# MLP up units in pairs of seven half-token products, with the down halves between them

## The chip, the cores and the metric

The kernel runs on one core of one Trainium2 chip. The time is device microseconds of one execution. The profiled execution is a run of its own, recorded by the hardware profiler.

## The reference

Two transformer blocks of different kinds on 512 tokens of width 1024, in float32. The first block (two layers: four-branch mixing and a gated FFN) is not touched. The second has a recurrent layer, a layer of banded attention, and behind each an MLP of this form, with 1024 inputs and 4096 hidden outputs:

```python
def rmsnorm_2(x, g):
    xf = x.astype(jnp.float32)
    y = xf * lax.rsqrt(jnp.mean(xf * xf, axis=-1, keepdims=True) + EPS)
    return (y * g.astype(jnp.float32)).astype(x.dtype)

def sqrelu_mlp(x, w_up, w_down):
    return jnp.square(jax.nn.relu(x @ w_up)) @ w_down

h = h + sqrelu_mlp(rmsnorm_2(h, mlp_norm[l]), w_up[l], w_down[l])     # l = 0, 1
```

## The kernel before

All weights lie in memory as 476 units of 128 x 1024 floats (512 KB): for most units eight 128 x 128 blocks, the weights of 128 outputs against 1024 inputs. Everything is transposed: a tile has 128 features on the partitions and 512 tokens in the columns. `X` holds the eight tiles of the residual. Float32 accuracy is made of three float32r products: `three` computes high x high, high weight x low value, low weight x high value, so a unit is 8 x 3 = 24 matmuls of 512 columns into one PSUM bank of `ps`.

A unit passes these stations, each engine in program order:
- SyncE loads it into one of four slots of `w_raw` when the unit four before has been used (`w_used`).
- ScalarE rounds it to `w_hi` (`split_weights`, L433; `tick(u)` does unit u + 2).
- GpSimd makes `w_lo` = raw - high in two halves of 512 (`low`, L368 and L370), in place of the raw weights.
- TensorE multiplies (`unit`, with `three` at L902 to L904), by `H_hi`, `H_lo` (the normed input) or `Y_hi`, `Y_lo` (the hidden tiles).
- ScalarE or DVE takes the bank away (`unit_out`).

An MLP (`mlp(n, U0)` on each engine) is four quarters of 8 up units and 8 down units. For an up unit ScalarE does the relu from PSUM to `fa` (L819), DVE multiplies by the row of inverse roots `RS` (L1980), squares it into `XS` (L1981), ScalarE rounds that to `Y_hi` (L821), DVE makes `Y_lo` (L1984). For a down unit DVE adds the bank to `X` (L1992). The gain is in `H`; the norm's root comes late, so RS is applied behind the up product: the norm is a matmul after unit 0 (L1026), a root on ScalarE (L477) and a reciprocal on DVE (L1484). Ahead of an MLP the eight output units of the layer are added to `X` (L1964 in the first), DVE sums the squares (L1476) and ScalarE and DVE make `H_hi` and `H_lo` (L455, L1489). The first block's scores (L1170) and the norm's sums per token (L1042) are plain float32 matmuls.

The middle quarters of an MLP run in a hardware loop on every engine, with the waits computed from the loop's counter. All order is written by hand.

Of the kernel before, what the change touches and what calls it, by code (L numbers as in the profile page):

```python
# [20 lines left out]
UNIT = 8 * P  # L21
WSLOTS = 4
# [16 lines left out]
QUARTERS = 4  # L39
U_AIN, U_AGATE, U_AOUT = 16, 2, DT  # L40
# [44 lines left out]
def build(nc, xT, w_all, vecs, cossin, win_fix, pool_w, sgu_wT, sgu_b, sgu_g, bias2, outT):  # L85
# [67 lines left out]

    o_rs2 = room(2 * KB)
# [26 lines left out]
    with ctx:  # L181
# [39 lines left out]
        stored = sem("stored")  # L221

# [96 lines left out]

        block = ctx.enter_context(nc.Block())  # L320
# [24 lines left out]
        def _(eng):  # L345
# [37 lines left out]
            def pooled(name):  # L383
# [12 lines left out]
                eng.sem_inc(sq_pooled, 1)  # L396
            at = 0
# [4 lines left out]
            lows(at, UO)  # L402
# [24 lines left out]
        def _(act):  # L427
# [374 lines left out]
            for k in range(3, DT):  # L802
                lru_hi(k)
            for k in range(1, DT):
                tick(UAO + k)
                x_tile("mlp0", "a_out")(k - 1)

            def mlp(n, U0):
# [4 lines left out]
                def quarter(i, first, last):  # L813
                    for j in range(8):
                        u = i * 16 + (U0 + j)
                        if j or not first:
                            tick(u, U0 + j)
                        act.wait_ge(w_used, u + 1)
                        nc.scalar.activation(fa[:, j % 2, :], ps[:, (U0 + j) % 4, :], ACT.Relu).then_inc(f_act, 1)  # L819
                        act.wait_ge(src_ready, i * 8 + (SRC[f"mlp{n}"] + j + 1))  # L820
                        nc.scalar.activation(Y_hi[:, j, :], XS[:, j % 2, :], ACT.Copy).then_inc(hi_ready, 1)  # L821
                    if last and n == 0:
                        tick_and_split(i * 16 + (U0 + 8), x_tile("kv_norm", "mlp0"))
                        return
# [73 lines left out]
        def _(pe):  # L898
            MM = nc.tensor.matmul

            def three(out, wh, wl, xh, xl, start, stop):
                MM(out, wh, xh, start=start, stop=False)  # L902
                MM(out, wh, xl, start=False, stop=False)  # L903
                return MM(out, wl, xh, start=False, stop=stop)  # L904
# [432 lines left out]

            def mlp(n, U0):
                def quarter(i, first):
                    for j in range(8):  # L1340
                        unit(i * 16 + (U0 + j), U0 + j, ps[:, (U0 + j) % 4, :], Hh, Hl, 8, i * 16 + (U0 + j - 3),
                             SPLIT[f"mlp_in{n}"] if first and j == 0 else None)
                        if first and j == 0:
                            norm(f"mlp{n}")
                    for m in range(8):
                        c = U0 + 8 + m
                        unit(i * 16 + c, c, ps[:, c % 4, :], Yh, Yl, 8, i * 16 + (c - 3), None if m else i * 8 + SPLIT[f"mlp{n}"])
                quarter(0, True)
                with pe.Fori(1, QUARTERS) as i:
                    quarter(i, False)  # L1350
# [880 lines left out]
```

## Time and profile before

| | us |
|---|---|
| median of three runs | 2755.32 (2753.72 to 2759.18) |
| profiled execution | 2752.11 |
| its span | 2750.4 |
| TensorE busy | 2708.3, 12398 matmuls |
| DVE, ScalarE, GpSimd busy | 1215.4, 1061.8, 1323.3 |

Granted TensorE clock over the span: 0.998. The kernel moves 259 MB at a mean of 94 GB/s. The first MLP runs from 1767 to about 2120 us, the second from about 2397 to the end. The records of TensorE are pipelined: a matmul of 512 columns is recorded with 0.39 us, so the distance of two starts is its cost, not its duration.

### The profile page before, as it was taken

The numbers are of one execution on the slowest core, as the hardware profiler recorded it, in microseconds if no ns is written. First come the engines' busy times: TensorE is split into PE (matmuls) and PEld (weight loads), VectorE is DVE, ScalarE is ACT, GpSimd is POOL, SyncE is SP. The second block draws the span as 40 slices with busy tenths as digits, with TensorE's granted clock in tenths as the row PEclk, the third lists the DMA queues.
The fourth block names the chain that finished last, engine by engine and source line by source line (L and its number), as shares of the span: only waits on it lengthen the run. The fifth ranks groups of instructions, "written<-read, shape, count | busy, mean of one in ns | idle before, by whom it ended". The sixth has DMA issues, their size and how long they took to land.

```text
span 2750.4 us, 34272 instructions
## 1 busy us (share of the span) xinstructions
PE 2708.3 (98%) x12398; PEld 2203.9 (80%) x12398; DVE 1215.4 (44%) x1603; ACT 1061.8 (39%) x1566; POOL 1323.3 (48%) x1028
## 2 busy tenths in 40 slices
PE   9999999999999999999999999999999998999999
PEld 7777787888877788787888877788888876788887
DVE  6755555222258645555121268633324237343222
ACT  4444434222343444434222348423324338433222
POOL 5455445544465545455444465454444432354443
PEclk9999999999999999999999999999999999999999
DMA  4233322233233333322323322223223220223233
GB/s 144 93 102 97 99 92 85 95 97 100 93 100 100 98 95 99 100 92 85 100 93 99 100 92 92 92 92 100 92 98 122 85 77 16 69 92 100 93 98 99
DMA packets 72699, 259.16 MB, mean 94 GB/s; under 512 B 8192, under 2 KB 9088, under 8 KB 72448
## 3 DMA queue, kind: packets, MB, share of 16 engines
q1 hardware_dynamic: 71280, 254.17, 29.0%
q10 hardware_dynamic: 1296, 3.28, 0.3%
q8 instruction: 87, 1.43, 0.2%
q14 instruction: 36, 0.29, 0.0%
HBM read 255.31 MB, written 2.10 MB: 94 GB/s over the span
## 4 chain that ended last, share of the span: by engine, by line
PE 67%; issue 13%; POOL 10%; DVE 5%; ACT 2%; DMA 1%; POOLq 0%; DVEq 0%; SPq 0%
PE ps L902 20%; PE ps L904 20%; PE ps L903 20%; POOL w_lo L370 6%; POOL w_lo L368 5%; PE ps L1170 1%; DVE XS L1981 1%; ACT w_hi L433 1%; DMA w_raw<-w_all 1%; DVE fb L1980 1%; PE ps L1065 1%; DVE st L1545 1%; PE ps L936 1%; PE ps L930 1%; PE ps L931 1%
## 5 line engine op out<-in xcount | busy, mean ns | idle before, releaser
L368 POOL TENSOR_TENSOR w_lo<-w_raw,w_hi 128x512 fp32r<-128x512 f32 x476 | 634.4, 1333 | 1327.1 <-ACT w_hi L433 1326.3
L902 PE MATMUL ps<-H_hi,w_hi 128*128 128x512 f32 x2160 | 858.4, 397 | 9.9 <-POOL w_lo L370 5.7
L904 PE MATMUL ps<-H_hi,w_lo 128*128 128x512 f32 x2160 | 841.4, 390 | 0.0
L903 PE MATMUL ps<-H_lo,w_hi 128*128 128x512 f32 x2160 | 841.0, 389 | 0.0
L433 ACT ACTIVATE w_hi<-w_raw 128x1024 fp32r<-128x1024 f32 x476 | 499.6, 1055 | 552.1 <-DMA w_raw<-w_all 551.8
L370 POOL TENSOR_TENSOR w_lo<-w_raw,w_hi 128x512 fp32r<-128x512 f32 x476 | 654.6, 1375 | 0.0
L902 PEld LDWEIGHTS ps<-H_hi,w_hi 128*128 128x128 f32 x2160 | 405.5, 188 | 109.8 <-issue 14.4
L903 PEld LDWEIGHTS ps<-H_lo,w_hi 128*128 128x128 f32 x2160 | 405.6, 188 | 89.2 <-issue 7.4
L904 PEld LDWEIGHTS ps<-H_hi,w_lo 128*128 128x128 f32 x2160 | 405.4, 188 | 85.3
L902 PE MATMUL ps<-Y_hi,w_hi 128*128 128x512 f32 x1168 | 457.8, 392 | 7.4 <-DVE Y_lo L1693 2.8
L904 PE MATMUL ps<-Y_hi,w_lo 128*128 128x512 f32 x1168 | 455.2, 390 | 0.0
L903 PE MATMUL ps<-Y_lo,w_hi 128*128 128x512 f32 x1168 | 454.9, 389 | 0.0
L902 PEld LDWEIGHTS ps<-Y_hi,w_hi 128*128 128x128 f32 x1168 | 219.6, 188 | 55.4 <-DVE Y_lo L1693 3.2
L904 PEld LDWEIGHTS ps<-Y_hi,w_lo 128*128 128x128 f32 x1168 | 219.5, 188 | 46.2
L903 PEld LDWEIGHTS ps<-Y_lo,w_hi 128*128 128x128 f32 x1168 | 219.7, 188 | 44.9
L1980 DVE TENSOR_TENSOR fb<-fa,RS 128x512 f32<-128x512 f32 x64 | 63.3, 989 | 147.0 <-ACT fa L819 113.3
L1992 DVE TENSOR_TENSOR X<-X,ps 128x512 f32<-128x512 f32 x48 | 33.0, 688 | 207.5 <-PE ps L904 207.5
L1813 DVE TENSOR_TENSOR XS<-fb,ps 128x512 f32<-128x512 f32 x44 | 30.3, 688 | 188.2 <-PE ps L904 177.8
L682 ACT ACTIVATE Y_hi<-XS 128x512 fp32r<-128x512 f32 x44 | 27.8, 632 | 218.3 <-DVE XS L1815 218.3
L1619 DVE TENSOR_TENSOR G<-ps,RS 128x512 f32<-128x512 f32 x64 | 44.3, 691 | 134.7 <-PE ps L904 132.8
L538 ACT ACTIVATE G<-G 128x512 f32<-128x512 f32 x64 | 40.3, 631 | 160.5 <-DVE G L1619 160.3
L821 ACT ACTIVATE Y_hi<-XS 128x512 fp32r<-128x512 f32 x64 | 40.5, 632 | 141.1 <-DVE XS L1981 141.1
(284 smaller groups left out, 2589.9 us busy)
## 6 DMA issues: line engine op xcount, KB each, us to landing
w_raw<-w_all SPq DMA_DIRECT2D x476, 512.0 KB, 3.5
X<-xT SPq DMA_DIRECT2D x8, 256.0 KB, 5.5
rel_bias<-bias ACTq DMA_DIRECT2D x1, 2048.0 KB, 8.9
outT<-X SPq DMA_DIRECT2D x8, 256.0 KB, 3.0
sguw<-sgu_wT ACTq DMA_DIRECT2D x2, 256.0 KB, 3.2
CS<-cossin SPq DMA_DIRECT2D x1, 256.0 KB, 7.7
sgub<-sgu_b ACTq DMA_DIRECT2D x2, 128.0 KB, 3.1
sgug<-sgu_g ACTq DMA_DIRECT2D x2, 128.0 KB, 3.2
```

The lines of the kernel that those rows point to most:

```text
L368: nc.gpsimd.tensor_tensor(w_lo[:, s, 0:UNIT // 2], w_raw[:, s, 0:UNIT // 2], f(w_hi[:, s, 0:UNIT // 2]), ALU.subtract).then_inc(w_lo_half, 1)
L370: nc.gpsimd.tensor_tensor(w_lo[:, s, UNIT // 2:UNIT], w_raw[:, s, UNIT // 2:UNIT], f(w_hi[:, s, UNIT // 2:UNIT]), ALU.subtract).then_inc(w ...
L433: nc.scalar.activation(w_hi[:, c % WSLOTS, :], w_raw[:, c % WSLOTS, :], ACT.Copy).then_inc(w_hi_ready, 1)
L538: nc.scalar.activation(dst, dst, ACT.Sigmoid).then_inc(sig_done, 1)
L821: nc.scalar.activation(Y_hi[:, j, :], XS[:, j % 2, :], ACT.Copy).then_inc(hi_ready, 1)
L902: MM(out, wh, xh, start=start, stop=False)
L903: MM(out, wh, xl, start=False, stop=False)
L904: return MM(out, wl, xh, start=False, stop=stop)
L1619: VE.tensor_tensor(dst, ps[:, bank(o), :], RS[:], ALU.mult).then_inc(g_lin, 1)
L1813: lk(VE.tensor_tensor(XS[:, j % 2, :], fb[:, j % 2, :], ps[:, (u0 + 2 * j + 1) % 4, :], ALU.mult))
L1980: lk(VE.tensor_tensor(fb[:, 0, :], fa[:, j % 2, :], RS[:], ALU.mult))
L1992: VE.tensor_tensor(X[:, m, :], X[:, m, :], ps[:, c % 4, :], ALU.add).then_inc(unit_out, 1)
```

## The change

In each MLP the first four up units stay as they are. The other 28 are taken in 14 pairs. Two units of 128 outputs, each with two halves of 512 inputs, against the two halves of 256 tokens, are a 2 x 2 block product: eight half products, made here of seven (Winograd's form of Strassen's scheme). For that,
- DVE makes four sums of weight halves a pair (S1 to S4, `weight_sum`), ScalarE their high parts (`hi_sum`), GpSimd their low parts, in `E_raw`, `E_hi`, `E_lo`;
- once for an MLP DVE makes four sums of token halves (`token_sums`, T0 to T3), the first two tiles of them between the additions of the layer before; their high parts are ScalarE's, their low parts DVE's (T3, T0) and GpSimd's (T1 ahead of the first pair, T2 behind it);
- partial results are copied from PSUM to `cp` by ScalarE and added by DVE (`c11`, `c12`, `c2`), then one DVE step does relu and RS, and ScalarE squares twice, into `XS` and `Y_hi`.

Down units hold two outputs against 4 input tiles each, and are computed as four half downs a window, two of them between the half products. A window is one pair of up units and two down units. At the end the down units of outputs 0 to 5 come as pairs of halves, 6 and 7 as whole units. The order of w_all follows. The rest of the kernel stays. The core of the diff, TensorE first:

```diff
+            def half_product(bank, wh, wl, xh, xl, fresh=True):
+                for k in range(4):
+                    c = slice(k * P, (k + 1) * P)
+                    m = three(ps[:, bank, 0:HS], wh[:, c], wl[:, c], xh(k), xl(k), fresh and k == 0, k == 3, not fresh)
+                return m
             def mlp(n, U0):
-                def quarter(i, first):
-                    for j in range(8):
-                        unit(i * 16 + (U0 + j), U0 + j, ps[:, (U0 + j) % 4, :], Hh, Hl, 8, i * 16 + (U0 + j - 3),
...
+                def window(i, w, first=False, last=False):
...
+                    half_product(BANK_Q, *slot_part(c + 1, 1), *half_of_h(4, 0))
...
+                    half_product(BANK_G, *slot_part(c, 1), *tokens(3)).then_inc(w_used, 1)
...
+                    half_product(BANK_R, *slot_part(c + 1, 0), *half_of_h(0, 0)).then_inc(w_used, 1)
...
+                    half_product(BANK_V, *sum_part(w, S1_), *tokens(0)).then_inc(st_mm, 1)
+                    if not (first or last):
+                        half_down(0)
+                    pe.wait_ge(st_lo, q * 3 + 1)
+                    pe.wait_ge(st_copy, q * 4 + 2)
...
+                    half_product(BANK_R, *sum_part(w, S2_), *tokens(1), fresh=False).then_inc(st_mm, 1)
+                    pe.wait_ge(st_lo, q * 3 + 2)
+                    pe.wait_ge(st_copy, q * 4 + 3)
+                    half_product(BANK_V, *sum_part(w, S4_), *half_of_h(4, 1), fresh=False).then_inc(st_mm, 1)
+                    if not (first or last):
+                        half_down(1)
+                    pe.wait_ge(st_lo, q * 3 + 3)
+                    pe.wait_ge(st_copy, q * 4 + 4)
...
+                    half_product(BANK_R, *sum_part(w, S3_), *tokens(2), fresh=False).then_inc(st_mm, 1)
+                    if not last:
+                        for d in range(0 if first else 2, 4):
+                            half_down(d)
```

ScalarE, one window and the start of an MLP:

```diff
+                def window(i, w, last=False):
+                    hi_unit(i, w, 3)
+                    copied(i, w, COPY_G)
+                    copied(i, w, COPY_R1)
+                    copied(i, w, COPY_V)
+                    if last:
+                        hi_unit(i, w, 4)
+                        hi_unit(i, w, 5)
+                    else:
+                        hi_second(i, w + 1)
+                        hi_unit(i, w, 5)
+                        hi_sum(i, w + 1, S1_)
+                        hi_sum(i, w + 1, S2_)
+                    copied(i, w, COPY_R2)
+                    if not last:
+                        hi_sum(i, w + 1, S4_, 2)
+                    squared(i, w, 0)
+                    if not last:
+                        hi_unit(i, w, 6)
+                    squared(i, w, 1)
...
+                relu(0)
+                tick(U0 + 1)
+                hi_tokens(3, 0)
+                relu(1)
+                up_hi(0)
+                hi_second(0, 0)
+                hi_unit(0, 0, 1)
+                hi_sum(0, 0, S1_)
+                hi_sum(0, 0, S2_)
+                hi_tokens(1)
+                hi_sum(0, 0, S4_, 2)
+                up_hi(1)
+                relu(2)
+                hi_unit(0, 0, 2)
+                up_hi(2)
+                hi_tokens(2)
+                relu(3)
+                up_hi(3)
+                for w in range(4):
+                    window(0, w)
```

DVE, one window and the start; GpSimd, the low parts of a pair:

```diff
+                def window(i, w, first=False, last=False):
+                    c11(i, w)
+                    if not last:
+                        weight_sum(i, w + 1, S1_)
+                        weight_sum(i, w + 1, S2_)
+                        if not first:
+                            down(i, w, 0)
+                        weight_sum(i, w + 1, S4_)
+                        weight_sum(i, w + 1, S3_)
+                    c12(i, w)
+                    linear(i, w, 0)
+                    if not (first or last):
+                        down(i, w, 1)
+                    low(i, w, 0)
+                    c2(i, w)
+                    linear(i, w, 1, 0 if first or last else 1)
...
+                token_sums(n, 2)
+                token_sums(n, 3)
                 link(root(f"mlp{n}", RS[:]))
...
+                up(0)
+                for o in (S1_, S2_):
+                    weight_sum(0, 0, o)
+                low_tokens(3, 1)
+                for o in (S4_, S3_):
+                    weight_sum(0, 0, o)
+                low_tokens(0, 2)
+                up(1)
+                up(2)
+                up(3)
```

```diff
+            def low_pair(n, U0, i, w):
...
+                eng.wait_ge(st_sum, q * 4 + 3)
+                nc.gpsimd.tensor_tensor(w_lo[:, s1, S:UNIT], w_raw[:, s1, S:UNIT], f(w_hi[:, s1, S:UNIT]), ALU.subtract).then_inc(w_lo_half, 1)
+                eng.wait_ge(st_sum, q * 4 + 4)
+                nc.gpsimd.tensor_tensor(w_lo[:, s2, S:UNIT], w_raw[:, s2, S:UNIT], f(w_hi[:, s2, S:UNIT]), ALU.subtract).then_inc(w_lo_half, 1)
+                nc.gpsimd.tensor_tensor(w_lo[:, s1, 0:S], w_raw[:, s1, 0:S], f(w_hi[:, s1, 0:S]), ALU.subtract).then_inc(w_lo_ready, 1)
+                for m, o in enumerate((S1_, S2_, S4_, S3_)):
```

## Rows read from the trace of the kernel before

**Rows 1.** The page: TensorE's busy time, and the chain that ended last, by engine.

```profile
PE 2708.3 (98%) x12398; PEld 2203.9 (80%) x12398; DVE 1215.4 (44%) x1603; ACT 1061.8 (39%) x1566; POOL 1323.3 (48%) x1028
...
PE 67%; issue 13%; POOL 10%; DVE 5%; ACT 2%; DMA 1%; POOLq 0%; DVEq 0%; SPq 0%
```

**Rows 2.** Windows view inside the first MLP: length, busy time and records of each engine.

```profile
core 0: us, PE busy (x) PEld busy (x) DVE busy (x) ACT busy (x) POOL busy (x), PEclk, DMA share, GB/s
...
1800.00:2100.00 300.00, 298.94 (x1319) 247.23 (x1318) 95.06 (x119) 94.91 (x120) 143.54 (x112) 1.00 0.30 96
```

**Rows 3.** TensorE's waits from 1700 us on: us in total, times, longest.

```profile
PE ps L902 <- DVE Y_lo L1984: 2.1, 2, 1.1
```

**Rows 4.** Timeline: start us, duration us; additions to X, then matmuls and loads.

```profile
1851.20 0.69 DVE L1992 TENSOR_TENSOR X<-X,ps 128x512 f32<-128x512 f32 x1 [4.75 <-PE ps L904]
1856.64 0.69 DVE L1992 TENSOR_TENSOR X<-X,ps 128x512 f32<-128x512 f32 x1 [4.75 <-PE ps L904]
...
1499.87 0.39 PE L902 MATMUL ps<-Y_hi,w_hi 128*128 128x512 f32 x1
1500.10 0.39 PE L903 MATMUL ps<-Y_lo,w_hi 128*128 128x512 f32 x1
...
1499.87 0.19 PEld L903 LDWEIGHTS ps<-Y_lo,w_hi 128*128 128x128 f32 x1
```

**Rows 5.** Timeline of the first block's float32 scores, by windows cut between the records.

```profile
112.23 0.38 PE L1170 MATMUL ps<-Kh,Qh 128*128 128x128 f32 x2
...
112.45 0.92 PE L1170 MATMUL ps<-Kh,Qh 128*128 128x256 f32 x3
...
112.67 0.70 PE L1170 MATMUL ps<-Kh,Qh 128*128 128x256 f32 x2
...
112.89 0.81 PE L1170 MATMUL ps<-Kh,Qh 128*128 128x384 f32 x2
```

**Rows 6.** Timeline of one-column float32 matmuls with a full weight load each.

```profile
435.97 0.47 PE L1042 MATMUL ps<-ones,SQ 128*128 128x1 f32 x3
...
436.42 0.36 PE L1042 MATMUL ps<-ones,SQ 128*128 128x1 f32 x2
```

**Rows 7.** Timeline of DVE and GpSimd in the first MLP's first quarter.

```profile
1781.76 1.28 DVE L1980 TENSOR_TENSOR fb<-fa,RS 128x512 f32<-128x512 f32 x1 [0.86 <-ACT fa L819]
1783.08 1.67 DVE L1981 TENSOR_TENSOR XS<-fb 128x512 f32<-128x512 f32 x1
...
1781.20 1.29 POOL L368 TENSOR_TENSOR w_lo<-w_raw,w_hi 128x512 fp32r<-128x512 f32 x1 [8.30 <-ACT w_hi L433]
1782.45 1.74 POOL L370 TENSOR_TENSOR w_lo<-w_raw,w_hi 128x512 fp32r<-128x512 f32 x1
```

**Rows 8.** Groups by line, 1800 to 2100 us, and the DMA issue to landing.

```profile
L370 POOL TENSOR_TENSOR w_lo<-w_raw,w_hi 128x512 fp32r<-128x512 f32 x56 | 73.8, 1319 | 0.0
...
L433 ACT ACTIVATE w_hi<-w_raw 128x1024 fp32r<-128x1024 f32 x57 | 59.6, 1052 | 96.7 <-DMA w_raw<-w_all 96.7
...
L1984 DVE TENSOR_TENSOR Y_lo<-XS,Y_hi 128x512 fp32r<-128x512 f32 x28 | 19.4, 693 | 20.2 <-ACT Y_hi L821 20.2
L821 ACT ACTIVATE Y_hi<-XS 128x512 fp32r<-128x512 f32 x28 | 17.7, 632 | 56.3 <-DVE XS L1981 56.3
...
w_raw<-w_all SPq DMA_DIRECT2D x55, 512.0 KB, 3.5
```

**Rows 9.** Timeline and chain where the first MLP begins.

```profile
1767.37 0.69 DVE L1964 TENSOR_TENSOR X<-X,ps 128x512 f32<-128x512 f32 x1 [2.39 <-PE ps L904]
...
1769.49 0.75 DVE L1489 SCALAR_TENSOR_TENSOR H_lo<-X,V,H_hi 128x512 fp32r<-128x512 f32 x1
1774.40 3.35 DVE L1484 RECIPROCAL RS<-SQ 128x512 f32<-128x512 f32 x1 [4.16 <-ACT SQ L477]
...
1772.71 0.88 PE ps L1026 x2
```

**Rows 10.** Groups by form, whole span: half-width operations on DVE and ScalarE.

```profile
L1755 DVE SCALAR_TENSOR_TENSOR vnT<-ps,st,sgug 128x256 f32<-128x256 f32 x8 | 3.9, 484 | 0.3
...
L619 ACT ACTIVATE SQ<-ps 128x256 f32<-128x256 f32 x8 | 3.1, 386 | 14.5 <-PE ps L1241 14.3
```

More of the change, by code:

```diff
@@ L21 @@
 UNIT = 8 * P
+HS = S // 2
+S1_, S2_, S4_, S3_ = range(4)
+COPY_G, COPY_R1, COPY_V, COPY_R2 = range(4)
+BANK_Q, BANK_G, BANK_V, BANK_R = 4, 5, 6, 7
 WSLOTS = 4
@@ L420, in _ @@
                     low(UO + 2 + (h > 4), 2 + (h > 4))
-            with eng.Fori(UO // WSLOTS + 1, NU // WSLOTS) as i:
-                for s in range(WSLOTS):
-                    low(i * WSLOTS + s, s)
+            lows(UO + 4, UM1 + 4)
+            low_mlp(1, UM1)
         @block.scalar
@@ new lines, in mlp @@
+                hi_tokens(1)
[7 more added lines that the diff above has]
+                up_hi(3)
+                for w in range(4):
+                    window(0, w)
+                with act.Fori(1, QUARTERS - 1) as i:
+                    for w in range(4):
+                        window(i, w)
+                window(QUARTERS - 1, 0)
@@ L833, in _ @@
+                window(QUARTERS - 1, 1, True)
+                split_weights(U0 + 62, U0 + 62)
+                for k in range(7):
+                    if n == 0:
+                        x_tile("kv_norm", "mlp0")(k)
+                    if k in (1, 3, 5):
+                        split_weights(U0 + 63 + k // 2, U0 + 63 + k // 2)
             mlp(0, UM0)
@@ new lines, in c11, with c12 @@
+                def c11(i, w):
+                    dve.wait_ge(st_copy, pair_at(n, i, w) * 4 + 2)
+                    VE.tensor_tensor(fa[:, 0, 0:HS], ps[:, BANK_Q, 0:HS], cp[:, COPY_R1, :], ALU.add).then_inc(st_c, 1)
+                def c12(i, w):
+                    q = pair_at(n, i, w)
+                    dve.wait_ge(st_copy, q * 4 + 4)
+                    dve.wait_ge(st_mm, q * 4 + 3)
+                    VE.tensor_tensor(fa[:, 0, HS:S], ps[:, BANK_V, 0:HS], cp[:, COPY_R2, :], ALU.add).then_inc(st_c, 1)
@@ new lines, in mlp @@
+                token_sums(n, 2)
+                token_sums(n, 3)
+                link(root(f"mlp{n}", RS[:]))
+                up(0)
[8 more added lines that the diff above has]
+                up(3)
+                for w in range(4):
+                    window(0, w, first=w == 0)
@@ new lines, in mlp @@
+                with dve.Fori(1, QUARTERS - 1) as i:
+                    for w in range(4):
+                        window(i, w)
+                window(QUARTERS - 1, 0)
+                window(QUARTERS - 1, 1, last=True)
+                for m, b in enumerate((2, 3, BANK_Q, BANK_G, 0, 1, 2, 3)):
+                    if m < 6 and m % 2 == 0:
+                        dve.wait_ge(d_mm, down_half(n, QUARTERS - 1, 1, 0) + m // 2)
+                    else:
+                        dve.wait_ge(w_used, U0 + (60 + m // 2 if m < 6 else 57 + m))
+                    VE.tensor_tensor(X[:, m, :], X[:, m, :], ps[:, b, :], ALU.add).then_inc(x_done, 1)
+                    dve.wait_ge(x_done, XDONE[f"mlp{n}"] + m + 1)
+                    if m not in (2, 4):
+                        dve.sem_inc(unit_out, 1)
```

339 lines of the change are left out of this document (271 added, 68 removed).

## Prediction

> **What bounds the kernel now.** I read the page's busy shares and chain first, then TensorE's windows inside the first MLP, then its waits, then the single starts. TensorE is busy 2708.3 of 2750.4 us, and two thirds of the chain that ends last is its matmuls [rows 1]. In the 300 us window inside the first MLP it is busy 298.94 us at granted clock 1.00, which is the 2.4 GHz level [rows 2]. All that the MLPs lose to a named wait is 2.1 us, one wait of about 1.1 us in each, where the first down unit needs the last part of `Y_lo` [rows 3]. So inside the MLPs the time is the number of matmuls times their spacing, and the change can gain only there.
>
> The spacing: two additions of down results to `X` start 5.44 us apart, one unit of 24 matmuls of 512 columns, 0.2267 us each. The records start 0.23 apart, and the load for the next matmul starts with the one before it and is hidden [rows 4]. 512 columns at 2.4 GHz are 0.2133, so each matmul carries 13 ns beyond its columns. A unit costs 5.44, a pair of up units 10.88 us.
>
> **What the change removes and adds on TensorE.** Per MLP four up units stay whole and 14 pairs are rewritten (28 pairs in all). A pair was 48 matmuls of 512 columns. It becomes seven half-token products of 4 contraction tiles x 3 parts = 84 matmuls of 256 columns. Down work is the same number of matmuls, regrouped. The price of one 256-column float32r matmul, c, decides: break-even is 10.88/84 = 129.5 ns. No such matmul is in the trace. Bounds:
> - From below: the scores of the first block are plain float32 and take two records a matmul, two clocks a column. Their 128-column records have the same time on the moving side (256 clocks, 107 ns) and a full 128x128 load each. Two of them take 112.23 to 112.45, 0.11 each; the 256-column ones next take 0.22 [rows 5]. One-column matmuls with a full load start 0.45/4 = 0.1125 apart [rows 6]: load and issue alone allow no less than 0.11.
> - Float32r's 13 ns: if it goes with the columns, c = 0.2267/2 = 0.1135. If it is a fixed price of each matmul, c = 0.1067 + 0.0133 = 0.120.
> - From above: if load and moving reads share something, so that time goes with 128 loaded + N moving elements, 640 elements now take 226.7 and 384 would take 136 ns.
>
> I take 0.120: the plain float32 records of three widths exceed their columns by about 3 ns whatever the width [rows 5], so a fixed price is the form that this trace shows. A pair is then 84 x 0.120 = 10.08, 0.80 saved; 28 pairs save 22.4 us. With 0.1135 it is 9.53, 37.8 saved; with 0.136 it is 11.42, 15 us lost.
>
> The records show loads hidden and short ones at 0.11 [rows 5, 6]. The Trainium skill ("TensorE: Matmul & The Clock Gate", Back-to-back issue gap) says that the single-matmul gap under-counts at small N in a stream of load and matmul pairs, 81 ns measured against 56 at N = 128. Were the same 25 ns added to its 262 cycles at N = 256, an estimate from that page, c would be 134 ns and the change would lose; no 256-column float32r stream is here to settle it.
>
> **The steady pair window, other engines.** A window of TensorE is 7 x 1.44 + 4 half downs x 2.72 = 20.96 us (two up units and two down units cost 21.76 before). GpSimd now makes 11 low parts of 512 a window (three halves of raw weights, four sums, four down halves), 8 before. DVE gets four weight sums, two linear steps, two `Y_lo`, four additions to `X` and four half-width additions; ScalarE about 10.3 us of work at 1.05 a unit and 0.63 a tile [rows 8]. DVE work with two SBUF inputs and GpSimd exclude each other: at the start of the MLP the square XS takes 1.67 instead of 0.69, exactly the rest of GpSimd's operation plus 0.56, and GpSimd's next takes 1.74 instead of 1.29 [rows 7]. GpSimd's two parts of a unit start 1.25 apart. The shared time is 11 x 1.25 + 8 x 0.5 = 17.8 us of 20.96, so it fits. The Trainium skill ("SBUF — State Buffer", on the shared port pair) calls it an exclusive lock for a whole instruction, for DVE operations with two SBUF inputs; the rows agree.
>
> I walked one window. Slots 0 and 1 come free at 2.9 and 4.3 us and land 3.5 later [rows 8]; ScalarE's high parts end at 8.9; the sums on DVE at 10.7; GpSimd makes the next window's seven low parts by 21.2 and the two parts for slot 2 by 24.2, 3.2 us into the next window, where its first half down starts at 5.8. The copies of banks G, R and V are done by 6.3, before 8.5. The chain of the second unit (sum, linear, square, low) ends 0.7 into the next window, used at 5.8. So no wait of TensorE in a steady window. That cover holds while 17.8 stays below 21; if GpSimd were the bound, each us of excess costs 28.
>
> **Where an MLP begins.** Here the new work meets on DVE and GpSimd. In trace time: unit 0 ends at 1772.7, the norm matmul takes 0.88 [rows 9], and three units of 5.44 end at 1789.9. DVE is done with the last `H_lo` at 1770.2 [rows 9]. Now come eight token sums of 256 columns at 0.48 [rows 10], two held up by GpSimd operations at 1770.4 to 1772.9: until 1776. The reciprocal of 3.35 [rows 9], which stood right behind the root, ends at 1779.5 (1777.8 before). up(0) 2.8, S1, S2, the low part of T3 (1024 wide, about 1.2) and S4: about 1786. From here GpSimd has the low part of T1 (2.5), seven parts of the first pair and T2 (2.5) ready without a gap; DVE has S3, T0 and eight steps up to the square of up(3), all with two SBUF inputs. By their order and [rows 7] they alternate at 1.25 + 0.5 = 1.75 a pair, so up(3)'s square ends near 1805.8. ScalarE is in order: only behind `up_hi(3)` (0.6) and `hi_unit` (1.05) come COPY_G and COPY_R1 (0.4 each by the 256-column row [rows 10]), done near 1808.3. TensorE waits for COPY_R1 ahead of the S2 product. It gets there near 1798 (1.4 late for the first low half, 1.0 for the next ones) and stands for 10.3 us. The S3 product waits for COPY_R2, which is queued behind the next pair's splits: 2.2 more. Sum 15 us, against 1.1 of before, in each MLP. If GpSimd held nothing up, the same chain would end at about 1798 and the sum would be 5 to 6.
>
> **Where an MLP ends.** The last window has no half downs between its products, and COPY_R2 stands behind two unit splits: ScalarE has them at 8.9 and the copy at 9.3, TensorE wants it at 8.4: 0.9 us. The last pair's Y chain (2 half additions, linear, two squares, low: about 4 us) lies beside one down unit of 5.44. Outputs 0 to 5 come 2.72 apart instead of 5.44, while DVE needs 2.9 each with the norm's steps, 1767.37 to 1770.24 [rows 9]; two full units at the end take the backlog up. Nothing for the reordering itself; the last two outputs come as before. The token sums inside the a_out and b_out units lie in DVE's idle time (over 2 us a unit [rows 9]).
>
> **Sum.** -22.4 + 2 x (15 - 1.1) + 2 x 0.9 = +7.2 us. The profiled execution took 2752.1 us (1.7 more than its span), 3.2 under the median of 2755.3; from the middle of both, 2753.7, I forecast 2761.
>
> **The rivals.**
> 1. The 13 ns goes with the columns, c = 0.1135: -37.8 + 29.6 = -8 us, faster, 2746. For it: the row's overhead is float32r's alone, and that type reads twice the elements in the same time. Against: the fixed 3 ns.
> 2. The start costs less: DVE or GpSimd do not alternate strictly, or the sums come earlier. 6.5 instead of 15: with c = 0.120 it is -22.4 + 10.8 + 1.8 = -10 us, 2744. For it: 10 of the 15 us hang on one in-order ScalarE queue. Against: [rows 7].
> 3. The narrow matmul costs over 0.125 (load and moving side in each other's way). Break-even with the start's loss is c = 0.117 ((10.88 - 29.6/28)/84); from there each ns costs 2.35 us. At 0.130 it is +30, 2784; at 0.136 +45. For it: nobody here runs a full load with 107 ns of float32r. Against: [rows 5, 6].
> 4. That the change does not do what it says (pairs that wait on each other): counted within 3.
>
> **How the numbers follow.** Forecast 0.38, rival 1 0.33, rival 2 0.13, rival 3 0.16. A measurement tells 0.2%, 5.5 us, from none. The forecast (+7, give or take 5) is faster 0.02, same 0.10, slower 0.26 of it; rival 1 (-8, give or take 5) 0.24, 0.08, 0.01; rival 2 0.09, 0.04, 0; rival 3 slower 0.16. Sums: 0.35, 0.22, 0.43. The likeliest's own range is 2753 to 2770. The range for 8 in 10 goes from rivals 1 and 2 together in part (-17) to a c of 0.129 (+28): 2737 to 2782.
>
> **What would show it.** The start distance of the new 256-column matmuls (0.120 against 0.1135 and 0.13); window length 21.0 us; TensorE's waits on ScalarE's `cp` near the start of each MLP, 10 us in one piece; DVE `XS` and sums at 1.2 to 1.7 there; no waits on `w_lo` or `E_lo` later. Wrong would be c off by more than 3 ns, a start that costs under 8, or waits in every window.

## The result, and the profile after

| | before | after |
|---|---|---|
| median, us | 2754.99 (2751.26 to 2759.18, 9 runs) | 2762.89 (2761.62 to 2766.03, 9 runs) |
| profiled execution, span | 2752.11, 2750.4 | 2763.11, 2761.4 |
| granted TensorE clock | 0.998 | 0.991 |

The ratio is 1.0031, 95% interval 1.0021 to 1.0042: slower, by 7.9 us. The page of the changed kernel:

```profile
PE 2702.9 (98%) x13406; PEld 2246.8 (81%) x13406; DVE 1403.9 (51%) x1863; ACT 1155.3 (42%) x1778; POOL 1501.3 (54%) x1116
...
PE 66%; issue 14%; POOL 11%; DVE 5%; ACT 2%; DMA 1%; POOLq 0%; SPq 0%; DVEq 0%; ACTq 0%
```

TensorE is busy 5.4 us less than in [rows 1], for 1008 more matmuls, but the span is 11 us longer. Of these, 0.8 us lie ahead of everything that was changed: the first matmul of the first MLP starts at 1767.90, against 1767.10 before. Its records where one window ends and where the next one ends (start us, duration us):

```profile
1890.29 0.39 PE L1085 MATMUL ps<-Y_hi,w_lo 128*128 128x512 f32 x1
1890.51 0.28 PE L1083 MATMUL ps<-H_hi,w_hi 128*128 128x256 f32 x1
1890.62 0.28 PE L1084 MATMUL ps<-H_lo,w_hi 128*128 128x256 f32 x1
1890.74 0.28 PE L1085 MATMUL ps<-H_hi,w_lo 128*128 128x256 f32 x1
...
1911.53 0.28 PE L1083 MATMUL ps<-H_hi,w_hi 128*128 128x256 f32 x1
```

The 256-column matmuls start 0.12 us apart, and a whole window takes 1911.53 - 1890.51 = 21.02 us. The same four units cost 4 x 5.44 = 21.76 before [rows 4]. So the steady part gains 28 x 0.74 = 20.7 us. TensorE's waits from 1700 us on (us in total, times, longest) show what is given back; [rows 3] had 2.1 us here:

```profile
PE ps L1083 <- issue: 16.1, 2, 8.9
...
PE ps L1083 <- POOL w_lo L456: 4.8, 2, 4.1
PE ps L1083 <- ACT cp L938: 3.2, 2, 1.9
```

All of this lies where the MLPs begin (4.1 and 7.3 us in the first, 0.8 and 8.9 in the second) and end (1.4 and 1.9). The windows view of the first MLP's start, with the columns of [rows 2]; the granted clock is the third number from the end:

```profile
1785.00:1790.00 5.00, 5.00 (x24) 4.14 (x23) 4.09 (x7) 4.32 (x6) 0.12 (x1) 1.00 0.31 105
1790.00:1795.00 5.00, 0.92 (x5) 0.42 (x3) 5.00 (x3) 1.06 (x1) 5.00 (x3) 0.86 0.35 107
1795.00:1800.00 5.00, 5.00 (x23) 5.00 (x24) 4.02 (x4) 2.06 (x3) 5.00 (x4) 0.50 0.00 0
1800.00:1805.00 5.00, 3.38 (x27) 3.18 (x25) 3.67 (x4) 2.06 (x3) 5.00 (x4) 0.96 0.54 165
1805.00:1810.00 5.00, 0.00 (x0) 0.00 (x0) 4.20 (x3) 1.58 (x3) 5.00 (x4) 0.73 0.11 45
1810.00:1815.00 5.00, 4.36 (x24) 4.39 (x25) 4.28 (x5) 3.70 (x8) 4.58 (x3) 0.59 0.01 2
```

TensorE stands idle for 4.1 us, and then five microseconds run at clock 0.50, the 1.2 GHz level: 23 matmuls instead of the 42 that 0.12 would allow. It stands for 7.3 us, and the clock is at 0.59 again. The start distances there are 0.21 to 0.22. Counted from the distances of all starts from 1780 to 1835 and 2410 to 2465, 75 matmuls are slowed, by 7.7 us in all.

The balance: -20.7 (windows) + 19.0 (21.1 of waits at the starts, less the 2.1 of before) + 3.3 (ends) + 7.7 (clock) = +9.3 us. Measured between the medians: +7.9; between the two profiled executions +11.0, of which 10.2 lie behind the start of the first MLP.

What TensorE waited for is seen on VectorE and GpSimd. First the timelines of both at the first MLP's start, then ScalarE's and one record of TensorE:

```profile
1756.95 1.40 DVE L2236 SCALAR_TENSOR_TENSOR T_raw<-X,V,T_raw 128x256 f32<-128x256 f32 x1
1758.27 1.51 DVE L2237 SCALAR_TENSOR_TENSOR T_raw<-X,V,T_raw 128x256 f32<-128x256 f32 x1
...
1771.93 0.75 DVE L1752 SCALAR_TENSOR_TENSOR H_lo<-X,V,H_hi 128x512 fp32r<-128x512 f32 x1
1772.71 0.48 DVE L2235 SCALAR_TENSOR_TENSOR T_raw<-X,V,T_raw 128x256 f32<-128x256 f32 x1
1773.23 1.38 DVE L2236 SCALAR_TENSOR_TENSOR T_raw<-X,V,T_raw 128x256 f32<-128x256 f32 x1
...
1780.27 3.34 DVE L1747 RECIPROCAL RS<-SQ 128x512 f32<-128x512 f32 x1
...
1790.45 3.38 DVE L2251 TENSOR_TENSOR T_lo<-T_raw,T_hi 128x1024 fp32r<-128x1024 f32 x1
...
1805.68 2.71 DVE L2258 TENSOR_TENSOR XS<-fb 128x512 f32<-128x512 f32 x1
...
1789.88 2.86 POOL L470 TENSOR_TENSOR T_lo<-T_raw,T_hi 128x1024 fp32r<-128x1024 f32 x1 [10.33 <-ACT T_hi L978]
1792.70 2.25 POOL L456 TENSOR_TENSOR w_lo<-w_raw,w_hi 128x512 fp32r<-128x512 f32 x1
...
1798.29 6.81 POOL L463 TENSOR_TENSOR E_lo<-E_raw,E_hi 128x512 fp32r<-128x512 f32 x4
...
1808.42 0.63 ACT L952 ACTIVATE Y_hi<-XS 128x512 fp32r<-128x512 f32 x1 [4.06 <-DVE XS L2258]
1808.96 1.04 ACT L525 ACTIVATE w_hi<-w_raw 128x1024 fp32r<-128x1024 f32 x1
1809.90 0.91 ACT L938 ACTIVATE cp<-ps 128x256 f32<-128x256 f32 x3
...
1810.64 0.55 PE L1083 MATMUL ps<-T_hi,E_hi 128*128 128x256 f32 x1 [7.26 <-issue]
```

From 1790 to 1808 VectorE and GpSimd mostly work by turns. The copies stand on ScalarE behind the rounding of up(3)'s square and the weight split (L525) after it. TensorE is free for its S2 product at 1803.4 and starts it at 1810.64. The profile names no releaser there ("issue"); that it is the copy, the second of three from 1809.90, is read from the times, and experiment 1 tests it.

### The profile page after: what moved, and what is told of

Its sections match the earlier page's. It is cut to its first block, busy times and chain, and to the rows that moved or that the text cites. A ratio compares the mean times of both kernels' runs of the same rounds, so it can differ in the third digit from the quotient of the medians.

```text
span 2761.4 us, 36893 instructions
## 1 busy us (share of the span) xinstructions
PE 2702.9 (98%) x13406; PEld 2246.8 (81%) x13406; DVE 1403.9 (51%) x1863; ACT 1155.3 (42%) x1778; POOL 1501.3 (54%) x1116
## 4 chain that ended last, share of the span: by engine, by line
PE 66%; issue 14%; POOL 11%; DVE 5%; ACT 2%; DMA 1%; POOLq 0%; SPq 0%; DVEq 0%; ACTq 0%
PE ps L1083 20%; PE ps L1084 19%; PE ps L1085 19%; POOL w_lo L423 5%; POOL w_lo L421 4%; DMA w_raw<-w_all 1%; PE ps L1351 1%; PE ps L1246 1%; DVE st L1808 1%; PE ps L1117 1%; PE ps L1111 1%; DVE ACC L1739 1%; PE ps L1112 1%; PE ps L1237 1%; DVE H_lo L1752 1%
## 5 line engine op out<-in xcount | busy, mean ns | idle before, releaser
L421 POOL TENSOR_TENSOR w_lo<-w_raw,w_hi 128x512 fp32r<-128x512 f32 x420 | 564.6, 1344 | 1048.0 <-ACT w_hi L525 1047.6
L1083 PE MATMUL ps<-H_hi,w_hi 128*128 128x512 f32 (+1 forms) x1936 | 748.2, 386 | 14.0 <-POOL w_lo L423 5.6
L1085 PE MATMUL ps<-H_hi,w_lo 128*128 128x512 f32 (+1 forms) x1936 | 731.0, 378 | 0.0
L1084 PE MATMUL ps<-H_lo,w_hi 128*128 128x512 f32 (+1 forms) x1936 | 730.7, 377 | 0.0
L525 ACT ACTIVATE w_hi<-w_raw 128x1024 fp32r<-128x1024 f32 x448 | 471.7, 1058 | 598.2 <-DMA w_raw<-w_all 597.7
L423 POOL TENSOR_TENSOR w_lo<-w_raw,w_hi 128x512 fp32r<-128x512 f32 x420 | 581.7, 1385 | 0.0
L1083 PEld LDWEIGHTS ps<-H_hi,w_hi 128*128 128x128 f32 x1936 | 365.0, 189 | 98.4 <-issue 13.9
L1084 PEld LDWEIGHTS ps<-H_lo,w_hi 128*128 128x128 f32 x1936 | 365.1, 189 | 72.8 <-issue 7.4
L1085 PEld LDWEIGHTS ps<-H_hi,w_lo 128*128 128x128 f32 x1936 | 364.8, 188 | 67.5
L463 POOL TENSOR_TENSOR E_lo<-E_raw,E_hi 128x512 fp32r<-128x512 f32 x112 | 178.5, 1623 | 0.0
L774 ACT ACTIVATE Y_hi<-XS 128x512 fp32r<-128x512 f32 x44 | 27.9, 633 | 218.4 <-DVE XS L2078 218.4
L1083 PE MATMUL ps<-T_hi,E_hi 128*128 128x256 f32 x336 | 96.5, 287 | 19.4 <-issue 16.1
L456 POOL TENSOR_TENSOR w_lo<-w_raw,w_hi 128x512 fp32r<-128x512 f32 x28 | 47.3, 1688 | 93.7 <-DVE E_raw L2282 93.7
```

The costliest lines, as they stand in the source:

```text
L421: nc.gpsimd.tensor_tensor(w_lo[:, s, 0:UNIT // 2], w_raw[:, s, 0:UNIT // 2], f(w_hi[:, s, 0:UNIT // 2]), ALU.subtract).then_inc(w_lo_half, 1)
L423: nc.gpsimd.tensor_tensor(w_lo[:, s, UNIT // 2:UNIT], w_raw[:, s, UNIT // 2:UNIT], f(w_hi[:, s, UNIT // 2:UNIT]), ALU.subtract).then_inc(w ...
L456: nc.gpsimd.tensor_tensor(w_lo[:, s1, S:UNIT], w_raw[:, s1, S:UNIT], f(w_hi[:, s1, S:UNIT]), ALU.subtract).then_inc(w_lo_half, 1)
L463: nc.gpsimd.tensor_tensor(sums_of(E_lo, w, o), sums_of(E_raw, w, o), f(E_hi[:, w % 2, o:o + 1, :]), ALU.subtract).then_inc(st_lo if m else ...
L525: nc.scalar.activation(w_hi[:, c % WSLOTS, :], w_raw[:, c % WSLOTS, :], ACT.Copy).then_inc(w_hi_ready, 1)
L1083: MM(out, wh, xh, start=start, stop=False, skip_group_check=resumed)
```

## The experiments

Ratios are to the kernel before on the same chip; after stands at 1.0031. All medians are of runs of the kernel named. Where two kernels' starts are compared matmul by matmul, times are counted from the first matmul of the MLP, since the executions reach it at different times (1765.6 to 1771.5 in the first MLP), for reasons ahead of the change.

**1. The order on ScalarE.** The first window's four copies are moved ahead of the last rounding and of the weight split behind it.

```diff
                 relu(3)
+                copied(0, 0, COPY_G)
+                copied(0, 0, COPY_R1)
+                copied(0, 0, COPY_V)
+                copied(0, 0, COPY_R2)
                 up_hi(3)
```

> The changed kernel with one move on ScalarE: in the first pair window of each MLP the four copies to cp stand right behind relu(3), ahead of up_hi(3) and the unit split. Theory A (the S2 product waits because the copies are queued behind the chain of up(3) on an in-order engine): in the first MLP the product starts at about 1805 instead of 1810.6, the first half down at about 1810.5 (when the last Y_lo of the four whole units is there) instead of 1816.5, so 5 to 6 us less in each MLP, 10 to 12 in all, 2751 to 2753 us. Rival B (the hidden units are late themselves, whatever the queue; the copies only look like the cause): the wait moves to the first half down and at most 3 us are won, 2760 or more.

Measured: 2752.06 us (2748.79 to 2755.92, 11 runs), ratio 0.9994 [0.9985, 1.0003]. Its waits of TensorE at the first MLP's start:

```profile
PE ps L1089 <- POOL w_lo L456: 4.1, 1, 4.1
PE ps L1089 <- issue: 2.5, 1, 2.5
```

The 7.3 us fell to 2.5 and the 8.9 of the second MLP to 3.2. Four lines in another place on one queue give 10.8 us back. By the distances of the starts, waits fell by 10.5 and the slowed matmuls from 7.7 to 5.7 us. This is the copies' position, not the amount of work.

**2. The clock by itself.** TensorE is kept busy in its two waits of each MLP's start with 256-column matmuls whose result nobody reads.

```diff
+                    if first:
+                        pe.wait_ge(unit_out, U0 + 1)
+                        fill((9, 1)[n])
                     pe.wait_ge(w_lo_half, u + 1)
...
+                    if first:
+                        fill((16, 20)[n])
                     pe.wait_ge(st_lo, q * 3 + 1)
```

> The changed kernel with matmuls on constants put into TensorE's two gaps at the start of each MLP (9 and 16 in the first, 1 and 20 in the second, 0.43 us each, into a free bank); nothing else moves. The granted clock falls to 0.50 after these gaps in the changed kernel, and some 50 narrow matmuls of the first MLP are 0.21 instead of 0.12 apart. Theory A (the low clock is a cost of its own on top of the waiting): 4 to 5 us less in the first MLP and 2 to 4 in the second, 2754 to 2757 us, with the granted clock near 0.998. Rival B (the clock costs nothing, since what follows the gap waits for other engines anyway): 2762 to 2765.

Measured: 2760.47 us (2757.99 to 2763.68, 8 runs), ratio 1.0025 [1.0014, 1.0035]. Its windows:

```profile
1795.00:1800.00 5.00, 5.00 (x37) 4.49 (x36) 4.13 (x3) 1.96 (x4) 5.00 (x4) 1.00 0.49 140
...
1810.00:1815.00 5.00, 4.25 (x30) 3.82 (x29) 4.91 (x5) 2.29 (x4) 4.31 (x4) 1.00 0.00 0
```

The clock stays at 1.00 in both starts. The median is 2.4 us lower than after's, between the two expectations, though the intervals of the two ratios overlap. The profiled execution is 5.1 us lower (2757.99 us), but 2.3 of that lie ahead of the first MLP. Matmul by matmul the two starts are 0.7 and 1.6 us shorter, 2.3 in all. So the 7.7 us of slowed matmuls are not 7.7 us of the total while the copies come as late as they do: a faster TensorE only reaches its wait earlier. What is back is what stood behind the last wait.

**3. VectorE and GpSimd in each other's way.** GpSimd's low parts of the first pair's weight sums and of T1 and T2 are cut to 2 columns; the rest of these low parts is left out, and TensorE multiplies the high parts in their place, so its work stays. GpSimd's low parts of the raw weights stay too.

```diff
-                    nc.gpsimd.tensor_tensor(T_lo[:, t, :, :], T_raw[:, t, :, :], f(T_hi[:, t, :, :]), ALU.subtract).then_inc(t_lo_g, 1)
+                    nc.gpsimd.tensor_tensor(T_lo[:, t, 0, 0:2], T_raw[:, t, 0, 0:2], f(T_hi[:, t, 0, 0:2]), ALU.subtract).then_inc(t_lo_g, 1)
```

> The changed kernel without GpSimd's share of the start: the low parts of the four weight sums of the first pair and of the token sums T1 and T2 are made for 2 columns only, and TensorE takes the high parts in their place (so for that one pair of each MLP part of the computation is left out); TensorE's work and DVE's instructions stay. Theory A (DVE and GpSimd hold each other up at the start): GpSimd has 7.5 us of operations less on the shared side, the square of up(3) comes 6 to 9 us earlier, and with the clock 8 to 11 us are won in each MLP, 2741 to 2747 us. Rival B (DVE's own chain of dependent steps sets the start): its steps take 0.69 instead of 1.7 but the order remains, under 3 us in each MLP, 2757 or more.

Measured: 2754.81 us (2752.14 to 2758.78, 10 runs), ratio 1.0006 [0.9996, 1.0015], 8 us less than after. In the first MLP the wait of 4.1 us fell to 1.9 and that of 7.3 to 6.5; in the second the 0.8 is gone and 5.9 are left of the 8.9. The first MLP's:

```profile
PE ps L1087 <- issue: 6.5, 1, 6.5
PE ps L1087 <- POOL w_lo L456: 1.9, 1, 1.9
```

T0's low part took 1.22 us on VectorE instead of 3.38, and up(3)'s square ended at 1802.23 against 1808.39 in after (of the 6.2 us between them, 1.4 lie ahead of the MLP). The gain is half of what theory A said, and more than rival B allowed. TensorE comes to its second wait earlier too, so that wait shrinks by less than the chain. The two engines' exclusion is real, and this part of it is worth 8 of the 27 us that the two starts cost (19.0 of waits and 7.7 of clock). The place of the copies is worth 10.8 by experiment 1. The two gains were not measured together, so how far they add up is open.

**4. The price of a narrow matmul.** In the kernel before, TensorE does 24 float32r products at each of five widths inside the first MLP, with the weights in place.

```diff
+                def probe():
...
+                    for N in (512, 384, 256, 128, 64):
+                        for r in range(2):
+                            for k in range(4):
+                                c = slice(k * P, (k + 1) * P)
+                                three(ps[:, 5, 0:N], w_hi[:, s, c], w_lo[:, s, c], H_hi[:, k, 0:N], H_lo[:, k, 0:N], k == 0, k == 3)
```

> The kernel before with a probe ahead of the second up unit of the first MLP: 24 float32r matmuls each of 512, 384, 256, 128 and 64 columns, full 128x128 loads, results not used. It gives the start distance c(N). Theory A (columns at 2.4 GHz plus a fixed price): 0.227, 0.173, 0.120, then 0.067 and 0.040 if load and issue allow. Theory A2 (the same, with a floor by the load): 0.111 to 0.12 at 128 and 64 columns as well. Rival B (the extra goes with the columns): 0.170 at 384 and 0.1135 at 256. Rival C (0.120 at 256 is the floor of the load and no fixed price): 0.12 at 256, 128 and 64 and 0.170 at 384. The time is about 18 us over the kernel before.

Measured: 2769.32 us, a single run, about 16 over the kernel before where 18 were expected. The first and the last record of 384, of 256 and of 128 columns:

```profile
1779.56 0.33 PE L902 MATMUL ps<-H_hi,w_hi 128*128 128x384 f32 x1
...
1783.57 0.33 PE L904 MATMUL ps<-H_hi,w_lo 128*128 128x384 f32 x1
1783.75 0.28 PE L902 MATMUL ps<-H_hi,w_hi 128*128 128x256 f32 x1
...
1786.49 0.28 PE L904 MATMUL ps<-H_hi,w_lo 128*128 128x256 f32 x1
1786.61 0.23 PE L902 MATMUL ps<-H_hi,w_hi 128*128 128x128 f32 x1
...
1789.13 0.28 PE L904 MATMUL ps<-H_hi,w_lo 128*128 128x128 f32 x1
```

23 steps each: 0.1743, 0.1191 and 0.1096 us. With 0.2267 at 512 columns, what stands over the columns at 2.4 GHz is 13.3, 14.3 and 12.4 ns at 512, 384 and 256: a fixed price. At 128 columns and at 64 (0.1104) a floor of 0.11 shows, twice the columns' 0.053. A split into 256 columns is just above that floor; one into 128 would have bought nothing.

**5. Sums first, all token low parts on VectorE.** DVE does all four weight sums and T3's low part ahead of the reciprocal; T1 and T2 go from GpSimd to DVE; copies as in experiment 1, COPY_R2 in its old place. ScalarE's roundings follow the new order.

```diff
+                weight_sum(0, 0, S1_)
+                low_tokens(3, 1)
+                for o in (S2_, S4_, S3_):
+                    weight_sum(0, 0, o)
                 link(root(f"mlp{n}", RS[:]))
                 up(0)
-                for o in (S1_, S2_):
-                    weight_sum(0, 0, o)
-                low_tokens(3, 1)
-                for o in (S4_, S3_):
-                    weight_sum(0, 0, o)
                 low_tokens(0, 2)
                 up(1)
+                low_tokens(1, 3)
                 up(2)
+                low_tokens(2, 4)
                 up(3)
```

> The changed kernel with the start of each MLP in another order, same arithmetic: the four weight sums of the first pair and the low part of T3 ahead of the reciprocal (so that GpSimd works while DVE is in the reciprocal, which takes one input), all four low parts of token sums on DVE (1.2 us instead of 2.8 on GpSimd), the copies G, R1, V ahead of the last squares on ScalarE. Theory (the start is set by DVE and GpSimd excluding each other and by the copies' place): the first wait of 4.1 us on the low weights goes, and of the 7 to 9 us before the S2 product under 3 are left; with the clock kept, 9 to 13 us less in each MLP, 2737 to 2746 us. Rival (what counts is the length of the up chain of the four whole units, which now starts behind the sums): the wait moves to the first half down, and under 6 us are won in each, 2751 or more.

Measured: 2769.13 us (2764.3 to 2773.07, 5 runs), ratio 1.0051 [1.0038, 1.0065]: no gain over after, and 6.2 us above it by the medians. DVE, then ScalarE's COPY_R2 and the S3 product that waits for it:

```profile
1785.11 0.69 DVE L2276 TENSOR_TENSOR E_raw<-E_raw,w_raw 128x512 f32<-128x512 f32 x1 [0.72 <-DMA w_raw<-w_all]
...
1787.05 3.34 DVE L1744 RECIPROCAL RS<-SQ 128x512 f32<-128x512 f32 x1
...
1814.43 0.36 ACT L931 ACTIVATE cp<-ps 128x256 f32<-128x256 f32 x1
...
1814.89 0.36 PE L1080 MATMUL ps<-T_hi,E_hi 128*128 128x256 f32 x1 [3.03 <-issue]
```

The wait on `w_lo` is gone, but the reciprocal ends at 1790.4 (1783.6 in after). Of these 6.8 us, 1.7 lie ahead of the MLP; the rest is the four sums and T3's low part that now stand ahead of it, with 0.7 us of waiting for a weight unit that the DMA has not brought yet and 0.5 for T3's high part. In the second MLP that waiting is 2.5 us.

TensorE, no longer held up before, waits 7.6 and 3.0 us in the first MLP, 7.6 and 3.7 in the second: 22.4 us with 0.3 and 0.2 on T0's low part, against 21.1 in after. The first of each pair is the wait for COPY_R1. It ends 36.8 us after the first MLP's first matmul, where it ended at 37.1 in experiment 1 and at 42.7 in after, so this product comes 6 us earlier than in after, but hardly earlier than the copies' place alone had brought it. In the second MLP it comes at 36.6, against 33.6 and 39.2: there the later start of the up chain shows. The second is a wait that neither after nor experiment 1 has: the S3 product waits for COPY_R2, which in its old place stands behind two and a half weight splits and two roundings of sums. Experiment 1 had moved that copy forward too. Between the 150th and the 200th matmul of each MLP, where this wait lies, experiment 5 loses 5.3 and 6.9 us to experiment 1, 12.2 of the 14.6 us that its two starts are longer.

Matmul by matmul the two starts are 0.3 us shorter and 2.9 longer than in after, 2.6 in all. The two profiled executions differ by 6.0: 1.7 more lie ahead of the first MLP, and 1.7 between the two starts. So what experiment 5 gains at the S2 product, 6 us and 2.6, the wait for COPY_R2 and the slowed matmuls around it take back. Neither expectation had asked for that copy.

**6. A shorter up chain.** Experiment 5's order, with the four whole units done as the pairs are: relu and RS in one DVE step from PSUM, ScalarE squaring twice. In the last window of an MLP COPY_R2 goes ahead of the last weight split.

```diff
+                def up_linear(j):
+                    dve.wait_ge(w_used, U0 + j + 1)
+                    VE.scalar_tensor_tensor(fb[:, j % 2, :], ps[:, (U0 + j) % 4, :], 0.0, RS[:], ALU.max, ALU.mult).then_inc(f_act, 1)
```

> As e5_order, and the four whole up units take DVE's single step from PSUM (maximum with zero, times RS) and two squares on ScalarE, as the pair windows do, so that two of three DVE steps on the shared side go; and COPY_R2 of the last window stands ahead of the last unit split. Theory: no wait over 1 us is left where an MLP begins, and the 1.4 to 1.9 us at its end go: 2 x (16.6 + 1.6) below the changed kernel, 2726 to 2732 us, 1% under the kernel before; 22.4 us from the matmuls and the rest from waits. Rival (e5_order has taken the gain and the clock is what is left): within 3 us of e5_order.

Measured: 2754.87 us (2750.41 to 2761.86, 11 runs), ratio 1.0003 [0.9994, 1.0012]. A miss by over 20 us, though 14 less than experiment 5. Its waits, then DVE and ScalarE:

```profile
PE ps L1075 <- ACT cp L931: 4.2, 1, 4.2
PE ps L1075 <- issue: 2.2, 1, 2.2
...
1795.73 1.75 DVE L2253 TENSOR_TENSOR Y_lo<-XS,Y_hi 128x512 fp32r<-128x512 f32 x1
1797.51 0.69 DVE L2247 SCALAR_TENSOR_TENSOR fb<-ps,RS 128x512 f32<-128x512 f32 x1
...
1798.24 0.63 ACT L941 ACTIVATE XS<-fb 128x512 f32<-128x512 f32 x1 [6.46 <-DVE fb L2247]
...
1799.29 0.91 ACT L931 ACTIVATE cp<-ps 128x256 f32<-128x256 f32 x3
```

ScalarE stood 6.46 us for the linear step of up(2), which was queued on DVE behind two token low parts and two `Y_lo`, and the copies stood behind that. I had counted the steps shorter but not asked what still stood ahead of the copies. The second wait, 2.2 us here and 2.1 in the second MLP, is again the S3 product's for COPY_R2, still in its old place: the copy ends at 1807.50, the product starts at 1807.59. Nor did the clock come back: 6.3 us of slowed matmuls remain. At the ends the waits of 1.4 and 1.9 us on COPY_R2 are gone, but 1.4 and 1.5 on the last `Y_lo` have taken their place.

**7 and 8. Room in the steady window.** One and three more GpSimd operations of 512 columns with two SBUF inputs in each window but the very first.

```diff
+                if not isinstance(q, int) or q:
+                    for r in range(3):
...
+                        nc.gpsimd.tensor_tensor(RS2[:], CS[:], CS[:], ALU.subtract).then_inc(t_more, 1)
```

> The changed kernel with one more GpSimd operation of 512 columns with two SBUF inputs in every pair window but the first, its result not used. By the count of the prediction (17.8 us of the shared side in a window of 21) the window has room for 1.25 to 1.75 more: 2761 to 2766 us, no change. Rival (the windows are as long as they are because DVE and GpSimd fill them, and 21.02 is that sum by chance): 27 x 1.3 = 35 us more, 2798.

> As e7_load1 with three more operations in every window. The shared side then holds 17.8 + 3 x 1.25 to 1.29 = 21.6 to 21.8 us for a window of 21.0: it should become the bound by 0.6 to 0.8 us a window and the kernel 15 to 25 us slower than the changed one, 2778 to 2790. If DVE's operations hold GpSimd up by more than 0.5 each, or chains across the two count, it is more, up to 3 x 1.75 - 3.2 = 2 us a window, 2818. If it stays at 2763 the count was too high.

Measured: with one 2764.28 us (6 runs), ratio 1.0037 [1.0025, 1.0049], the same as after; with three 2774.61 us (4 runs), 1.0067 [1.0052, 1.0083], less than the 2778 to 2790 expected. Windows 1850 to 2050, after and then the kernel with three:

```profile
1850.00:2050.00 200.00, 200.00 (x1266) 181.87 (x1265) 111.15 (x153) 89.46 (x145) 151.63 (x105) 1.00 0.31 103
...
1850.00:2050.00 200.00, 197.92 (x1236) 178.45 (x1235) 116.86 (x149) 86.73 (x139) 183.27 (x133) 1.00 0.30 98
```

TensorE is busy for all 200 us in after. With three more operations GpSimd is busy 92% and TensorE begins to wait. The count of the prediction, 17.8 us of shared time a window, gives 19.1 with one (below 21.0: nothing) and 21.6 with three: 27 windows x 0.6 = 16 us over after. Measured is 0.36% of the time, 10 us. So the steady window has room for one such operation and not for three, about 3 us by this count, and the time lost is not there.

**9. Both corrections joined.** From experiment 6: the reciprocal goes ahead of S2, the sum that waits for the DMA; the copies and the weight splits ahead of them go ahead of square_up(2), COPY_R2 ahead of square_up(3); the linear steps stand as early as their buffers allow.

```diff
+                square_up(0)
+                square_up(1)
+                hi_tokens(1)
                 hi_tokens(2)
+                hi_unit(0, 0, 2)
+                hi_unit(0, 0, 3)
+                copied(0, 0, COPY_G)
+                copied(0, 0, COPY_R1)
+                copied(0, 0, COPY_V)
+                square_up(2)
+                copied(0, 0, COPY_R2)
+                square_up(3)
```

> Both corrections joined at the start of each MLP: the four whole up products are read from PSUM by VectorE's max-and-scale step (0.69 us, not slowed there) and squared twice on ScalarE, all token low parts go to VectorE, the reciprocal stands ahead of the second weight sum, and the first window's copies with the third weight split go ahead of square(2), COPY_R2 ahead of square(3). From e6's trace: the copies could follow the V product at 1795.83 and be done by about 1797.0 instead of 1800.0, so the wait before R2 falls from 4.2 to 1 to 1.5 us, the second wait (2.2 us, the third unit's low part behind the late split) falls below 1, per MLP 4 us less than in e6, two MLPs 8 us, and the granted clock has no gap of 4 us left in front of it. Theory A (the start's waits are queue order on ScalarE and VectorE, and all that is left of them falls to it): e6's 2754.9 less 8 = 2745 to 2750, ratio to before 0.996 to 0.998. Theory B (the time that e6 keeps over the sum lies elsewhere, in VectorE and GpSimd shutting each other out, so that T1's low part at about 1796 takes the place of the copies): 2752 to 2756, with a wait on DVE T_lo of 2 us or more before R2.

Measured: 2740.19 us (2736.41 to 2741.47, 5 runs), ratio to before 0.9944 [0.993, 0.9958]: 13.2 us faster than before, 0.9% faster than after. The kernel leaves nothing out. It beats the interval of theory A. TensorE's starts behind a wait in the first MLP, then two windows of it:

```profile
1803.46 0.36 PE L1077 MATMUL ps<-T_hi,E_hi 128*128 128x256 f32 x1 [0.51 <-DVE T_lo L2245]
...
1806.79 0.47 PE L1077 MATMUL ps<-Y_hi,w_hi 128*128 128x512 f32 x1 [1.67 <-issue]
...
1800.00:1805.00 5.00, 4.49 (x37) 4.24 (x35) 4.82 (x4) 4.33 (x8) 5.00 (x4) 1.00 0.34 109
1805.00:1810.00 5.00, 3.33 (x16) 2.72 (x15) 4.83 (x5) 0.63 (x1) 4.54 (x3) 1.00 0.02 5
```

Of 11.4 us of waiting 2.2 are left, of 9.7 in the second MLP 1.7. No stretch of either start is below clock 1.00, and of the slowed matmuls 0.2 us remain. Against experiment 6 the waits are 12.7 - 3.9 = 8.8 us less and the slow matmuls 6.3 - 0.2 = 6.1: together 14.9, measured between the medians 14.7. I had expected the 8 of the waits alone. The expectation had also put the second wait down to the third unit's low part; experiment 6's trace has it on COPY_R2, which is moved here. That the clock counts in full here, and did not in experiment 2, fits with nothing waiting behind it; it was not varied by itself in this order.

Against before the balance is -20.7 (windows) + 3.9 - 2.1 (starts) + 2.9 (the ends, now on the last `Y_lo`) = -16.0; measured -13.2. In the two profiled executions the difference is 10.8, but this kernel's reaches the first MLP 4.4 us later (1771.48 against 1767.10), with a wait of 3.1 us on `Y_lo` in the unchanged recurrent layer ahead of it. From the first MLP to the end it is 15.2 us shorter, which leaves 0.8 of the balance unplaced.

## Why the prediction came out as it did

The time was right (2761 forecast, 2762.9 measured) and so was its sign. Step by step:

- **The price of a 256-column matmul: right.** 0.120 from the fixed form of the 13 ns, against 0.120 in the windows and 0.119 in experiment 4. This term carried 0.33 of the chances on the other side (0.1135) and 0.16 above. The argument from [rows 5] chose well. The estimate from the Trainium skill ("TensorE: Matmul & The Clock Gate", Back-to-back issue gap), 134 ns, is not borne out by either trace.
- **The window: 20.96 forecast, 21.02 measured.** The 28 pairs saved 20.7 instead of 22.4 us.
- **No waits in steady windows: right**, and experiments 7 and 8 show with how much room.
- **The start, 15 us in each MLP: right in place, not in its parts.** Waits are 11.4 and 9.7 us. The queue named (copies on ScalarE behind the last rounding, and that behind VectorE and GpSimd alternating) is the one that experiment 1 undoes. But 10.3 us of it were to come in one piece and 2.4 on low halves; the trace has 7.3 and 4.1, 8.9 and 0.8. In the first MLP the copies were done 2.3 us later than forecast, but TensorE came to them 5.4 us later (1803.4 for 1798), held up by the first wait and the clock, and so stood for less. The further 2.2 on COPY_R2 did not show (the clock, below).
- **The step that failed: the token sums.** I put those of the a_out units into "DVE's idle time", at no cost. Each of their tiles took about 3.9 us under GpSimd's operations instead of 4 x 0.48, since two of its four steps took 1.4 and 1.5. The last `H_lo` started at 1771.93, 2.4 us later than in [rows 9]; the execution was up to 0.9 us late before these sums, so about 1.5 is theirs. The eight sums behind it took 7.6 us for 5.8 forecast, with four of them held up, not two. So the reciprocal ended at 1783.6 against 1779.5 forecast.
- **The step that was missing: the clock.** Both waits were forecast, and that TensorE would come out of them at 0.50 was not asked. Waits 9 us smaller than forecast (21.1 for 30) and 7.7 us of slowed matmuls nearly cancelled; the sum is better than its terms, and that much of the agreement is luck. The two hang together: at full clock TensorE would have reached its waits earlier and stood longer, as experiment 2 shows. So does the missing wait on COPY_R2: the S2 product before it ran at 0.21 a matmul, time for the copy, and in experiment 2, at full clock, 0.75 us of waiting stood there, of 2.2 forecast. Once the product before it came early, in experiments 5 and 6, the wait was 3.0 to 3.7 and 2.2 us.
- **The ends: 0.9 forecast, 1.4 and 1.9 measured**, on COPY_R2 behind two splits as said.
- **Rival 2** (a start that costs 6.5, 2744) did not come, but experiment 9 went past it: 2.2 and 1.7 us of waits, 2740.

## What to carry to other kernels

A rewrite that saves matmuls in a steady loop pays only if its first pass is ordered as well as its loop. Walk each in-order queue at the start and ask of every copy that frees a bank what stands ahead of it, and whether that itself waits for another engine. Do this for every such copy: with COPY_R1 early and COPY_R2 left behind, experiment 5 gained nothing. Put ahead of such a copy only what is already there, and keep off the front of the queue any operation that waits for a transfer (2.5 us in experiment 5's second MLP). A wait of TensorE of several microseconds is followed by slowed matmuls. Filling the wait gave back little here (2.3 us of 7.7), taking it away gave back both (14.9 us for 8.8 of waiting in experiment 9).

## What the runs showed of the hardware

- Float32r matmuls with a full weight load each start at 0.2267, 0.1743, 0.1191, 0.1096 and 0.1104 us for 512, 384, 256, 128 and 64 columns: about 13 ns over the columns down to a floor of 0.11.
- TensorE came out of waits of 4.1, 7.3 and 8.9 us at granted clock 0.50 to 0.60 and was back at 1.00 by 1815 and 2450. With fillers in the waits, and in experiment 9 with waits of 0.5 and 1.7, it stood at 1.00 throughout both starts.
- A VectorE step that reads PSUM and one SBUF input kept its 0.69 us while GpSimd was busy (experiments 6 and 9), where steps with two SBUF inputs took 1.75. The Trainium skill ("SBUF — State Buffer", SBUF: two separate sides) names, of VectorE's operations, those in a two-port mode and those with two SBUF inputs as taking the exclusive lock. The rows agree for two SBUF inputs; the two-port mode was not looked at. Taking an operand from PSUM was thus a way out of the lock here.
- A low part 1024 wide took 1.22 us on VectorE alone, 3.38 when GpSimd was in one of its own of 2.86.
